# Moved waits in the attention passes and a recurrence grouped by kind of product

## The reference, cut to what matters

```python
# stick-breaking attention, per head and block of 128 queries
z = q @ k.T * scale
log_keep = where(mask, log_sigmoid(-z), 0.0)
suffix = cumsum(log_keep, reverse=True) - log_keep
w = where(mask, exp(log_sigmoid(z) + suffix), 0.0)
out = w @ v
...
# gated linear attention, per chunk; g: log gates, b: their running sum
o = A @ v + (q * exp(b)) @ S
S = exp(b_last) * S + (k * exp(b_last - b)).T @ v
...
o = rmsnorm(o) * silu(r)
```

## Time and profile before

| | us |
|---|---|
| three timed runs | 2964.31, 2964.82, 2969.36 (median 2964.82) |
| profiled execution, own time | 2952.34 |
| its span | 2950.8 |
| TensorE busy | 2792.1 (95%) |
| VectorE, ScalarE, GpSimd busy | 1384.2, 960.7, 139.8 |
| four attention passes, 675.4 to 1091.6 | 111.6, 103.0, 102.5, 99.1 |
| gated linear attention from its first level, 1921.4 to 2110.0 | 188.6 |

### The profile page before, as it was taken

The page is one execution under the profiler, slowest core; times in us unless marked ns, Lnnn a source line. Parts: engine busy times, 40 slices in busy tenths (PEclk is TensorE's granted clock), DMA queues, the critical chain, the costliest instruction groups (busy, mean ns, idle before and its releaser), DMA issues.

```text
span 2950.8 us, 35931 instructions
## 1 busy us (share of the span) xinstructions
PE 2792.1 (95%) x14762; PEld 2299.6 (78%) x14762; DVE 1384.2 (47%) x1818; ACT 960.7 (33%) x1567; POOL 139.8 (5%) x231
## 2 busy tenths in 40 slices
PE   5999999998899899998999899998999999999998
PEld 4778888886676678655898667876798988989888
DVE  7666556555555552574525481367334223232223
ACT  6453222335556562122213251233223112031122
POOL 0101111110000001000010000000000000000000
PEclk7999999999999999999999899898799999999999
DMA  2222332332211114320342001000121111111112
GB/s 95 101 92 93 115 113 91 111 122 78 72 53 50 68 57 161 125 114 29 100 135 93 29 1 43 30 29 1 49 81 50 44 44 44 57 43 44 44 56 81
DMA packets 128553, 209.25 MB, mean 71 GB/s; under 512 B 6013, under 2 KB 106538, under 8 KB 124826
## 3 DMA queue, kind: packets, MB, share of 16 engines
q1 hardware_dynamic: 109610, 144.79, 14.7%
q0 software_dynamic: 18800, 62.38, 6.0%
HBM read 161.02 MB, written 46.14 MB: 70 GB/s over the span
## 4 chain that ended last, share of the span: by engine, by line
PE 86%; DVE 6%; ACT 4%; issue 2%; DVEq 1%; ACTq 1%; DMA 0%; SPq 0%; POOL 0%
PE ps L428 23%; PE ps L422 20%; PE ps L1854 19%; PE ps L1951 4%; PE ps L1995 2%; PE ps L2007 2%; PE ps L1935 2%; PE ps L2194 2%; PE ps L1910 2%; PE ps L2261 2%; PE ps L2276 1%; PE ps L2074 1%; PE ps L1864 1%; PE ps L1921 1%; PE ps L2161 1%
## 5 line engine op out<-in xcount | busy, mean ns | idle before, releaser
L428 PE MATMUL ps<-a_hi,w_hi 128*128 128x512 f32 x736 | 295.6, 402 | 4.7 <-issue 3.5
L407 DVE TENSOR_TENSOR w_lo<-w_raw,w_hi 128x2048 fp32r<-128x2048 f32 x60 | 137.5, 2291 | 345.6 <-ACT w_hi L403 345.6
L428 PE MATMUL ps<-a_lo,w_hi 128*128 128x512 f32 x736 | 293.2, 398 | 0.0
L403 ACT ACTIVATE w_hi<-w_raw 128x2048 fp32r<-128x2048 f32 x60 | 114.9, 1914 | 543.2 <-DMA w_raw<-in_w_ff 364.7
L428 PE MATMUL ps<-a_hi,w_lo 128*128 128x512 f32 x736 | 290.9, 395 | 0.0
L422 PE MATMUL ps<-w_hi,f_lo 128*128 128x256 f32 x1024 | 290.0, 283 | 0.0
L422 PE MATMUL ps<-w_lo,f_hi 128*128 128x256 f32 x1024 | 290.0, 283 | 0.0
L422 PE MATMUL ps<-w_hi,f_hi 128*128 128x256 f32 x1024 | 289.9, 283 | 0.0
L1367 DVE TENSOR_TENSOR proj_out<-ps,proj_out 128x512 f32<-128x512 f32 x210 | 142.0, 688 | 240.2 <-PE ps L1854 240.2
L1854 PE MATMUL ps<-t_hi,pw_hi 128*128 128x512 f32 x480 | 196.1, 409 | 3.7 <-DVE t_lo L1341 3.7
L422 PEld LDWEIGHTS ps<-w_hi,f_hi 128*128 128x128 f32 x1024 | 196.7, 192 | 0.2
(11 more groups left out here) (342 smaller groups left out, 5737.7 us busy)
## 6 DMA issues: line engine op xcount, KB each, us to landing
w_raw<-in_w_ff SPq DMA_DIRECT2D x32, 1024.0 KB, 5.5
pw_raw<-in_w_in SPq DMA_DIRECT2D x30, 1024.0 KB, 5.5
projections<-proj_out POOLq DMA_DIRECT2D x88, 256.0 KB, 3.4
w_raw<-in_w_in SPq DMA_DIRECT2D x20, 1024.0 KB, 5.2
projections<-proj_sq POOLq DMA_DIRECT2D x32, 256.0 KB, 2.7
w_raw<-in_w_out SPq DMA_DIRECT2D x8, 1024.0 KB, 5.5
x_in<-in_x SPq DMA_DIRECT2D x8, 512.0 KB, 5.0
q<-projections SPq DMA_DIRECT2D x4, 1024.0 KB, 4.8
```

The costliest lines, as they stand in the source:

```text
L403: act.activation(W_hi[s][:, :, :], W_raw[s][:, :, :], ACT.Copy).then_inc(w_hi, 1)
L407: dve.tensor_tensor(W_lo[s][:, :, :], W_raw[s][:, :, :], W_hi[s][:, :, :].bitcast(f32), ALU.subtract).then_inc(w_lo, 1)
L428: last = pe.matmul(bank[banks[j]][:, :], w[s][:, k, ct * P:(ct + 1) * P], a[:, k, t0 + th * HALF:t0 + (th + 1) * HALF], start=(k == 0 and ...
```

## The change

In the attention passes: the wait for the values goes from the start of a pass to its first weighing; the first filler runs before the score product of step 2 and no longer behind it; the ScalarE halves of the weight split go from behind the softplus terms (steps 1, 2, 10, 11) to before them (2, 3, 10, 11); the VectorE halves go from the end of steps 3, 4, 12, 13 to before the scan of steps 4, 5, 12, 13; the copy of the attended block goes behind the subtraction. The split of the first filler's weights goes up into the last projection.

In the gated linear attention: the keys are turned into banks 2 and 3 (not 6, 7 and 2) before the last piece of gate product; the eight updates are issued in a row into eight halves of banks 2, 3, 0 and 1; the 16 AA products follow, then the 16 state products, with four state tiles in place of two. The norm tiles of the first pair lie in the weight area, its outputs are gated after the operands of the second pair's level 1, and the exponential of that level goes ahead of the norm.

```diff
@@ ScalarE
@@ projection
                 proj_first(n, 2)
+                if n == NPROJ - 1:
+                    split_hi(act, L1, 0)
@@ attention pass
                     if S - 1 in fill_after:
                         keep_filler(fill_after[S - 1])
+                    if S in (2, 3):
+                        half_hi(n + 1, 1, S - 2)
+                    if S in (10, 11):
+                        half_hi(n + 2, 0, S - 10)
                     if S < 14:
                         softplus_terms(S + 2, S)
                     else:
                         keep_first(S)
-                    if S in (1, 2):
-                        half_hi(n + 1, 1, S - 1)
-                    if S in (10, 11):
-                        half_hi(n + 2, 0, S - 10)
@@ gated linear attention
                 mix_gates_after(p, NL - 2)
+                act.wait_ge(kt_done, p + 1)
+                act.activation(KTM[:, :], bank[3][0:META, 3 * P:4 * P], ACT.Copy)
+                act.activation(KTK[:, 0:TT - 1, :], wide(2, (TT - 1) * P)...).then_inc(kt_ok, 1)
                 mix_gates_after(p, NL - 1)
-                act.wait_ge(kt_done, p + 1)
-                act.activation(KTK[:, :, :], wide(6)...)
-                act.activation(KTM[:, :], bank[2][0:META, 0:P], ACT.Copy).then_inc(kt_ok, 1)
...
                 if p:
                     keep_mix_gate(1, 2)
+                else:
+                    level_exp(1, 1)
@@ VectorE
@@ attention pass
+                    dve.drain()
+                    dve.tensor_tensor(C[S % 2][:, 0:w], wide(4 + 2 * (S % 2), w), C[S % 2][:, 0:w], ALU.subtract).then_inc(z_used, 1)
                     if S - 2 in pair_after:
                         keep_attended(pair_after[S - 2])
-                    dve.drain()
-                    dve.tensor_tensor(C[S % 2][:, 0:w], wide(4 + 2 * (S % 2), w), C[S % 2][:, 0:w], ALU.subtract).then_inc(z_used, 1)
                     if S >= 1:
                         keep_second(S - 1)
+                    if S in (4, 5):
+                        half_lo(n + 1, 1, S - 4)
+                    if S in (12, 13):
+                        half_lo(n + 2, 0, S - 12)
                     if S < 15:
                         suffix_sum(S + 1)
@@ gated linear attention
+            def gate_outputs(p):
+                for th in range(2):
+                    dve.wait_ge(mg_ok, 1 if p == 0 else 2 + th)
+                    for h in range(2):
+                        dst = OUT[:, 2 * p + h, th * HALF:(th + 1) * HALF]
+                        dve.tensor_tensor(as_gate(p, dst), as_gate(p, GNT[p][2 * h + th][:, :]), mix_gate(p, 2 * th + h), ALU.mult).then_inc(go_kept, 1)
...
-                    if t >= 2:
-                        dve.wait_ge(go_done, 8 * p + t - 1)
+                    if t >= 4:
+                        dve.wait_ge(go_done, 8 * p + t - 3)
@@ TensorE
@@ attention pass
-                pe.wait_ge(v_in, 16 * i + 16)
-                for j in range(4):
-                    pe.wait_ge(*c_kept(NPROJ - 1, j))
+                pe.wait_ge(*v_kept(NPROJ - 1))
...
+                    if S == 0:
+                        filler(first, early)
                     if S < 14:
                         scores(S + 2)
-                    filler(first, early)
+                    if S:
+                        filler(first, early)
+                    else:
+                        pe.wait_ge(*c_kept(NPROJ - 1, 3))
@@ gated linear attention
+                for t in range(TT - 1):
+                    pe.transpose(wide(2)[:, t * P:(t + 1) * P], KE[1][:, t * P:(t + 1) * P], ident[:, :])
+                pe.transpose(bank[3][0:META, 3 * P:4 * P], KEM[:, :], ident[:, :]).then_inc(kt_done, 1)
+                mix_gate_part(p, mix_upto[p][NL - 2], mix_upto[p][NL - 1])
+                pe.wait_ge(kt_ok, p + 1)
+                for t in range(TT):
+                    if t == 4:
+                        pe.wait_ge(lv_kept, 16 * p + 2 * NL)
+                    ... update of block t into update_out(t)
+                for h in range(2):
+                    if h:
+                        pe.wait_ge(mg_raw, (4, 6)[p])
+                    for t in range(TT):
+                        pe.matmul(attended(t, h), GV[:, t, (2 * p + h) * P:(2 * p + h + 1) * P], AA[:, TT * h + t, :], start=(t % 4 == 0), stop=False)
                 for t in range(TT):
                     pe.wait_ge(st_ok, 8 * p + t + 1)
                     for h in range(2):
                         half = slice(64 * h, 64 * h + 64)
+                        last = pe.matmul(attended(t, h), GS[t % 4][half, h * P:(h + 1) * P], QE[1][half, t * P:(t + 1) * P], start=False, stop=(t % 4 == 3))
```

More of the change, by code:

```diff
@@ L191, in build @@
     KTK = at("ktk", [P, TT, P], off=lr_at)
+    wgu_at = pos[0]
     wgu = work("wgu", [16, 256])
+    KTM = at("ktm", [META, P], off=wgu_at)
     lvl = work("lvl", [P, len(GLA_LEVELS), P])
@@ L197, in build @@
     restart = work("restart", [P, SEQ])
-    GS = [at(f"gs{u}", [P, 256], off=pos[0] - SEQ * 4 + u * 1024) for u in range(2)]
-    KTM = at("ktm", [META, P], off=pos[0] - SEQ * 4 + 2048)
+    GS = [at(f"gs{u}", [P, 256], off=pos[0] - SEQ * 4 + u * 1024) for u in range(4)]
+    GNT = [[at(f"gla_norm{j}", [P, HALF], off=w_at + j * HALF * 4) for j in range(4)], NB]
     GT = [at(f"gt{u}", [P, HALF], off=out_at + u * HALF * 4) for u in range(2)]
@@ L1720, in mix_lo @@
                                   ALU.subtract).then_inc(m_lo, 1)
+            def gate_outputs(p):
[4 more added lines that the diff above has]
+                        dve.tensor_tensor(as_gate(p, dst), as_gate(p, GNT[p][2 * h + th][:, :]), mix_gate(p, 2 * th + h), ALU.mult).then_inc(go_kept, 1)
+                    if th == 0:
+                        for j in range(4):
+                            dve.sem_inc(kept[j], 1)
+                        if p:
+                            mix_lo(0, 2)
             from_ref(0, GLA_LEVELS[0])
@@ L2288, in gla_sums @@
                     pe.wait_ge(gn.rs, 4 * p + j - 1)
-                pe.matmul(bank[2 + j % 2], ones[:, :], NB[j][:, :], start=True, stop=True).then_inc(gn.ss, 1)
+                pe.matmul(bank[2 + j % 2], ones[:, :], GNT[p][j][:, :], start=True, stop=True).then_inc(gn.ss, 1)
             level_and_gate(0, 0)
             for p in range(2):
-                if p:
-                    pe.wait_ge(go_kept, 4)
-                for v in range(1, NL):
-                    level_and_gate(p, v)
+                for v in range(1, NL - 1):
+                    if p and v == 1:
+                        pe.wait_ge(gn_read, 2)
+                        level(p, v)
+                        pe.wait_ge(gn_read, 4)
+                        mix_gate_part(p, mix_upto[p][0], mix_upto[p][1])
+                    else:
+                        level_and_gate(p, v)
@@ L2297, in _ @@
+                level(p, NL - 1)
                 pe.wait_ge(lv_kept, 16 * p + 2 * NL - 2)
-                pe.wait_ge(mg_raw, (4, 6)[p])
                 pe.wait_ge(qe_ok2, p + 1)
-                for t in range(TT):
-                    pe.transpose(wide(6)[:, t * P:(t + 1) * P], KE[1][:, t * P:(t + 1) * P], ident[:, :])
-                pe.transpose(bank[2][0:META, 0:P], KEM[:, :], ident[:, :]).then_inc(kt_done, 1)
-                pe.wait_ge(kt_ok, p + 1)
-                def update(t):
-                    if t >= 2:
-                        pe.wait_ge(st_ok, 8 * p + t - 1)
+                for t in range(TT - 1):
+                    pe.transpose(wide(2)[:, t * P:(t + 1) * P], KE[1][:, t * P:(t + 1) * P], ident[:, :])
@@ L2310, in update, with attended @@
                     else:
[L2311 to L2313 removed]
+                        pe.matmul(update_out(t), KTK[:, t - 1, :], GV[:, t - 1, p * 256:(p + 1) * 256], start=True, stop=True).then_inc(u_done, 1)
+                def attended(t, h):
+                    return bank[4 + 2 * h + t // 4][:, (t % 4) * P:(t % 4 + 1) * P]
+                for h in range(2):
[3 more added lines that the diff above has]
+                        pe.matmul(attended(t, h), GV[:, t, (2 * p + h) * P:(2 * p + h + 1) * P], AA[:, TT * h + t, :], start=(t % 4 == 0), stop=False)
```

73 lines of the change are left out of this document (32 added, 41 removed).

## The result

The changed kernel takes **2894.44 us** (median of four, 2893.10 to 2895.61), the kernel before on the same chip 2964.57 (2964.01 to 2969.36): ratio 0.976, 95% interval 0.9743 to 0.9777. Forecast were 2904 us and faster; the time is 9.6 us under the forecast and inside the range. The profiled execution took 2895.61 us (span 2893.7, mean granted clock 0.973), 57.1 us of span less than before. By stages: attention passes 27.2 us (forecast 18.2), gated linear attention 24.0 (forecast 30.8), the stages between them, which the change doesn't touch, 5.1, the rest 0.8. So the sum came out well because two misses of opposite sign lie in it.

A forecast was written before the change was run, and what follows sets the result against it. TensorE, busy nearly all the span, was taken to bound the kernel. Gains of 30.8 (gated linear attention), 2.4, 14.4 and 1.4 sum to 49.0 us; 2952.3 less these, with 0.8 of offset kept, gave 2904 us, range 2890 to 2924.

The forecast's parts named there:

- The change between 128 and 64 rows: GLA recurrences: each change of row count costs about 0.2 us; grouping leaves two in place of 32.
- The second recurrence returns to the full clock: Recurrence of the second head pair: new order fills the idle time before it, 32.1 us become 11.9, gain 20.2.
- the wait of about 2 us before the level product: Behind the first recurrence: the level product waits for VectorE's two operand products, loss 1.9 us.
- all five waits: Third attention pass: 3.4 us moves behind the filler, 0.85 and 1.4 stay at steps 11 and 14, two others go.
- the three terms: Attention passes: 2.4 us from the early filler, 14.4 from the new order, 1.4 from the first pass's early split.
- State products do run side by side: Rival, GLA recurrences: state products run in pairs, up to 1.7 us less in each, 2901 us; chance 0.06.
- Between there and the next recurrence VectorE sets the pace ... and TensorE's clock doesn't matter.: GLA levels between the recurrences: VectorE's copies and operations bound them; a 0.3 us loss was allowed just before.
- The order: Attention passes: later weight splits and subtraction before the attended copy remove waits, 3.6 us a pass, 14.4 in four.
- the start terms: Attention passes: filler before the third score product gains 2.4 us in three passes, first pass's early split 1.4.
- slower, by the clock in the passes: Rival, attention passes: short work behind the moved 3.4 us wait leaves the clock low, 2974 us; chance 0.02.
- an offset that stays: Rival: the 12.5 us between profiled and timed runs are not of the recurrence and stay, 2915 us; chance 0.17.
- 11.7 of the 12.5 us of offset: First recurrence: timed runs have it at the low clock, costing 11.7 us of their excess over the profiled run.

The follow-up runs named there:

- e5_alternate: Changed kernel with AA and state products again by turns for each block and head, behind the grouped updates: 2897.46 us, ratio 0.9784 to the kernel before.
- e8_keep_clock: Changed kernel plus 35 products of 512 columns between the recurrences, whose results nobody reads: 2891.06 us, ratio 0.9762 to the kernel before.
- e4_start_only: Kernel before with only the passes' early filler, early value split and wait for values at the first weighing: 2959.75 us, ratio 0.9995.
- e1_attn_only: Kernel before with only the edits to the attention passes: 2930.86 us, ratio 0.9899.
- e2_gla_only: Kernel before with all edits except those to the attention passes: 2922.33 us, ratio 0.9859.
- e3_order_only: Kernel before with only the passes' new VectorE and ScalarE order (subtraction first, weight splits later): 2937.25 us, ratio 0.9911.
- e7_pair_levels: Changed kernel with the two heads of a level by turns for each block: 2892.93 us, ratio 0.9772 to the kernel before.
- e10_gate_between: Changed kernel with needed gate matmuls between the recurrences plus 10 unread products, 7 gate matmuls a level kept: 2893.68 us, ratio 0.9780 to the kernel before.
- e9_third_gate: Changed kernel plus 35 unread products between the recurrences, 24 gate matmuls moved from behind the second recurrence into levels: 2882.65 us, ratio 0.9756 to the kernel before.

## Why the prediction came out as it did

**Right, with its number.** The change between 128 and 64 rows costs 0.2 us: AA products 0.223 in a row, 0.42 by turns (e5_alternate). The second recurrence returns to the full clock: window 10.56 us at 1.00, and from the last level to the gate matmuls 20.7 us were won where 20.2 were forecast; the gate matmuls behind took 5.79 (5.8), 1.75 less (1.7). The wait for the turned keys is gone, the wait of about 2 us before the level product is there. In the third pass all five waits are as forecast, three left and two gone, and in the four passes the waits are 17 us less against the 18.2 of the three terms. The halves add up.

**Rival that held.** State products do run side by side (chance given 0.06): 1.09 us for four blocks in place of 1.7, then VectorE's states bind. It is worth 0.6 us in a recurrence, not 1.7. The Trainium skill's "TensorEngine Tiling (Array Packing)", Key Properties, says that a change of tiling mode drains the engine; the trace agrees in that each change has a price (0.42 against 0.22), and doesn't show the drain itself. The Trainium skill's "TensorE: Matmul & The Clock Gate", Why this matters for your kernels, says that matmuls in distinct row groups run concurrently; the trace agrees (2.06 against 3.43 us a level).

**Step that failed:** "Between there and the next recurrence VectorE sets the pace ... and TensorE's clock doesn't matter." It was read from a stretch in which the clock was full for most levels; the one level at the low clock in it (6.48 us) was passed over. At the low clock a level with its seven gate matmuls takes TensorE 6.48 + 3.28 = 9.8 us against VectorE's 6.0. Two such levels in the profiled execution made 3.6 us of loss where 0.3 were allowed, and level(1,0) with 6.30 us and the norm's sums took 3.3 more than the sum had. Those 6.6 us, with 0.75 of clock in the levels of p = 0, less the 0.6 that the second recurrence gave beyond its terms, are the miss of 30.8 against 24.0. e8_keep_clock shows it by giving time back with no change but added matmuls: 4.2 us up to level(1,1), 4.7 up to the end of the second recurrence.

**Term that was mis-sized:** the passes, 27.2 for 18.2. The order is the large part: 23.8 us alone where 14.4 were forecast; the start terms gave 3.7 for 3.8, but only behind the order. The idle time came as forecast (17.1 for 18.2). What the sum had at nothing is TensorE's busy time, 10.3 us less for the same matmuls. Some 6 us of it are clock: TensorE's work inside the low stretches of the passes was 20.3 us before and is 8.7 now, and half of the difference is 5.8. The fillers have all of that: the low clock lay on filler matmuls for 17.1 us before and for 0.1 now. In the kernel before such a stretch lies right behind the 3.44 us wait of the third pass (from 894.2); the changed kernel has a wait of 3.37 there and no low stretch, so the wait's length alone doesn't settle it. The other 4 to 5 us belong to no kind of matmul: line by line they differ by less than 2 us beyond the clock, so most of it would be more overlap between neighbours, with 21 waits for other engines where there were 32. No run isolates this.

**Rival seen in part:** *slower, by the clock in the passes* (chance given 0.02). The changed kernel doesn't show it, but e4_start_only does at a small size: the filler ahead of the score product brought 5.4 us more of TensorE's work under the low clock, which took back 2.7 of the 3.2 us won.

**Luck:** the median came out 9.6 us under the forecast because 9.0 us too much in the passes, 5.9 in stages that the change doesn't touch (5.1 of them between the passes and the gated linear attention, at a mean clock of 0.96 for 0.95) and some 2 of the offset between profile and median outweigh the 6.8 that the gated linear attention fell short. That the time lies so near is no proof of the terms. (Where the prediction prices an offset that stays, its own terms give 2916 us and not 2915.) The prediction gave 11.7 of the 12.5 us of offset to the first recurrence at the low clock. The offset is gone (the median is now 1.2 below the profiled time), it stays with e1_attn_only and goes with e2_gla_only within 4 us, and the stretch and its price were seen in e3_order_only. Yet e1_attn_only has an execution at the full clock there that isn't faster for it, so that this stretch makes the whole offset isn't shown.

## What to carry to other kernels

Group matmuls by the number of rows that they use, and let neighbours use different halves of the rows: 0.2 us for each passage and 40% of a level's time are at stake. A stall on TensorE can cost the clock behind it as well as its own length, so ask of each stretch not only which engine sets its pace but which would at the half clock, and try needed matmuls in the idle times. A local gain of some microseconds is easily covered in the total by the clock of stages with the same code (e7_pair_levels, e10_gate_between), so read it from the stage. When both engines are within some tenths of a microsecond of each other, speeding up one gives only the difference: 0.3 us a level of the 1.4 at p = 0 in e7_pair_levels.

## What the runs showed of the hardware that was not expected

More work made a stretch shorter: 35 added matmuls of 512 columns took 4.2 us off 21.3 (e8_keep_clock). 13 us more of products in the two recurrences cost some 3 us in all (e5_alternate). And waits of one or two microseconds went with a fall of the clock: in the levels of p = 1 it fell behind 1.54 us (e8_keep_clock) and behind 1.79 us (e10_gate_between) of idle time, and once for 3.4 us behind waits of 0.56 and 0.47 (e8_keep_clock, from 1981.3), while in e9_third_gate it held behind 0.40 and 0.84, at 1.00 for 43.70 us. The Trainium skill's "TensorE: Matmul & The Clock Gate", A second HAM failure mode: psum-queue depth-cycling, says that short idle times between groups of matmuls make the clock swing. The traces agree in part: 0.77 against 1.00 in those levels, but in e7_pair_levels 0.9 to 2.1 us of idle time before each of four levels left the clock at 1.00. No run tells what decides between the two. Runs of one kernel differ by 3 to 13 us with their mean clock, which is more than most single edits are worth.
